# Five projections of a second layer as block products, and what then stands beside its banded attention

## The reference

```
h    = rmsnorm(x, norm1_g);  proj = h @ w_in
qa, ka, va, qm, km, vm, om, gm, mg = split(proj)     # 512,128,128, 512,512,512,512, 16, 2048
ya   = windowed_gqa(rmsnorm(qa)*gain/8, rmsnorm(ka)*gain, va, bias, sink)   # 8 heads of 64, 2 kv heads,
                                                     # 128 queries against the blocks before, at, after
qm,km = silu(conv5(concat(qm, km)) + b)              # 5 taps along the tokens, one channel at a time
ym   = rmsnorm(mlstm_fwd(qm,km,vm,gm) + mlstm_bwd(...)) * sigmoid(om)
g    = sigmoid(mg + merge_b)
x    = x + (g[:1024]*(ya @ w_branch_attn) + g[1024:]*(ym @ w_branch_mlstm)) @ w_out
x    = x + moe(rmsnorm(x))                           # 32 experts, two a token
```

## Time and profile before

| | |
|---|---|
| median of three runs | 1687.57 us |
| the profiled execution | 1688.09 us |
| its span, first to last instruction | 1686.3 us |
| mean granted TensorE clock | 0.993 |
| PE busy | 1630.7 us (97%) |
| DVE busy | 737.4 us (44%) |
| ACT, POOL busy | 387.8 (23%), 192.5 us (11%) |
| chain that ended last | PE 87%, DMA 8%, DVE 2% |

### The profile page before, as it was taken

One profiled execution on the slowest core, in us unless ns is written; L12 is line 12 of the kernel. 1 busy time (PEld: TensorE's weight loads), 2 busy tenths in 40 slices (PEclk: granted clock), 3 DMA queues, 4 the chain that ended last, 5 costly groups with the idle time before them and its releaser, 6 DMA issues.

```text
span 1686.3 us, 18096 instructions
## 1 busy us (share of the span) xinstructions
PE 1630.7 (97%) x7006; PEld 947.7 (56%) x7006; DVE 737.4 (44%) x1526; ACT 387.8 (23%) x823; POOL 192.5 (11%) x206
## 2 busy tenths in 40 slices
PE   7999999999999999999999999999999999997986
PEld 4444454578888888875444678744633333333332
DVE  3387786455454535451677256325521121121211
ACT  4443663510000000022365224100511111111110
POOL 1000000000000000010000424115022222221221
PEclk9999999999999999999999999999999999999999
DMA  5531114030222222223111111636899999999996
GB/s 189 125 75 50 51 51 140 11 113 0 100 78 72 100 100 75 106 66 117 50 50 50 51 50 51 206 97 234 352 394 417 416 418 417 424 413 417 422 416 235
DMA packets 75138, 303.63 MB, mean 180 GB/s; under 512 B 13037, under 2 KB 14194, under 8 KB 62124
## 3 DMA queue, kind: packets, MB, share of 16 engines
q1 hardware_dynamic: 64432, 287.40, 43.3%
q0 software_dynamic: 9872, 12.91, 3.7%
q10 hardware_dynamic: 748, 2.15, 0.3%
HBM read 306.99 MB, written 15.73 MB: 191 GB/s over the span
## 4 chain that ended last, share of the span: by engine, by line
PE 87%; DMA 8%; DVE 2%; SPq 2%; issue 1%; ACT 0%; POOL 0%; POOLq 0%; DVEq 0%; ACTq 0%
PE ps L1216 11%; PE ps L1260 11%; PE ps L1665 11%; PE ps L1084 9%; PE ps L1357 7%; PE ps L1504 6%; PE ps L1682 5%; DMA W<-in_w_expert_up 5%; PE ps L1120 3%; PE ps L1080 3%; PE ps L1543 3%; PE ps L1569 3%; DMA W<-in_w_expert_down 2%; PE ps L1368 2%; PE ps L1139 1%; SPq L766 1%
## 5 line engine op out<-in xcount | busy, mean ns | idle before, releaser
L3017 DVE SCALAR_TENSOR_TENSOR smb<-smb,ptb,ps 64x512 f32<-64x512 f32 x34 | 38.2, 1124 | 273.9 <-ACT smb L2139 273.9
L1084 PE MATMUL ps<-W 128*128 128x512 f32 (+1 forms) x336 | 149.3, 596 | 1.9 <-DMA W<-in_w_in 1.9
L1665 PE MATMUL ps<-W,cmask 128*64 128x512 f32 x480 | 132.5, 609 | 4.6 <-DMA W<-in_w_expert_up 3.9
L1665 PE MATMUL ps<-W,gb 128*64 128x512 f32 x480 | 129.5, 599 | 2.8 <-DMA W<-in_w_expert_up 2.7
L1357 PE MATMUL ps<-W 128*128 128x512 f32 x272 | 122.3, 599 | 1.9 <-DVE yT L2657 1.9
L1216 PE MATMUL ps<-yT,W 128*128 128x256 f32 x512 | 113.0, 379 | 0.0
L1682 PE MATMUL ps<-W,ptb 128*64 128x512 f32 x464 | 106.0, 598 | 4.2 <-DVE ptb L3023 3.3
L1260 PE MATMUL ps<-W,mix 128*128 128x256 f32 x496 | 108.5, 379 | 0.0
L1216 PEld LDWEIGHTS ps<-yT,W 128*128 128x128 f32 x512 | 97.3, 190 | 13.2
L1084 PEld LDWEIGHTS ps<-W 128*128 128x128 f32 (+1 forms) x336 | 61.2, 188 | 75.3 <-issue 72.9
L1260 PEld LDWEIGHTS ps<-W,mix 128*128 128x128 f32 x496 | 94.3, 190 | 12.8
(11 more groups left out here) (479 smaller groups left out, 2433.4 us busy)
## 6 DMA issues: line engine op xcount, KB each, us to landing
W<-in_w_expert_up SPq DMA_DIRECT2D x25, 2048.0 KB, 34.8
W<-in_w_expert_down SPq DMA_DIRECT2D x24, 2048.0 KB, 33.4
W<-in_w_expert_gate SPq DMA_DIRECT2D x22, 2048.0 KB, 32.0
W<-in_w_in SPq DMA_DIRECT2D x16, 2048.0 KB, 7.7
W<-in_w_up SPq DMA_DIRECT2D x8, 2048.0 KB, 8.3
W<-in_w_down SPq DMA_DIRECT2D x8, 2048.0 KB, 7.7
W<-in_w_out SPq DMA_DIRECT2D x4, 2048.0 KB, 7.8
W<-in_w_expert_gate SPq DMA_DIRECT2D x8, 1024.0 KB, 21.8
```

Of the source, the lines that this page charges most:

```text
L1084: ins = pe.matmul(ps[0:n, bank, :], wv[:, k, j * P:j * P + n], hT[:, k, :], start=(k == 0), stop=(k == KT - 1))
L1665: ins = pe.matmul(ps[64 * part:64 * part + 64, 2, :], xsT[s][:, k, :], w[part][:, k, :], start=(k == 0), stop=(k == KT - 1))
```

## The change

Nine projections (QM, KM, QA, VM, OM, and the four merge ones) now share one list of 63 block products, numbered `n`, and the names begin with `side_`: `side_product`, `side_keep`, `side_post`, `side_w_sums` and `side_h_sum` do what those with `gate_` did. `G2` keeps only `va2` (2) and `knorm`. Products 0 to 24 (QM, KM, QA, and four products of VM) come before the attention, `N_AHEAD = 25`; the other ten (VM's last three and OM) stand beside its steps; 35 to 62 are the merge ones, where they were. The convolutions and the gate scans now stand on DVE among the posts of products 4 to 18, and the first tap of each convolution is on ACT (`tap`), a copy with a scale. The roots of the query norms are taken of 16 columns a pair of chunks: `pair_sums` sums the squares to one column a head and tile of tokens, `pair_std` and `pair_recip` work on them, and `spread_roots` spreads the reciprocals over the partitions. The keys keep the old way. The `hT` sums now live in `x`, so `x` is stored to HBM after the norm and loaded again after the last product. Two small loads at the start of the kernel move under another semaphore.

```diff
+        side_h = [parts(x[:, n, :]) for n in range(4)]
+        early_w = [parts(flat(ptb[:, :, :])), parts(flat(yT[:, 6:8, :]))]
+        gate_w = [[parts(flat(smb[:, 2 * n:2 * n + 2, :])) for n in range(2)] + [parts(flat(yT[:, 4:6, :]))],
...
+        side_tmp = 3 * [[mix[:, 0, 512:1024], mix[:, 1, 512:1024], mix[:, 2, 512:1024], mix[:, 0, 0:512]]]
+        side_tmp += 2 * [[stage[:, 1, 0:512], stage[:, 1, 512:1024], stage[:, 0, 0:512], stage[:, 0, 512:1024]]]
+        side_tmp += 2 * [[yT[:, 0, :], yT[:, 1, :], yT[:, 2, :], R[:, 15376:15888]]]
+        side_tmp += 2 * [[R[:, 8208 + 512 * n:8720 + 512 * n] for n in range(4)]]
+        side_out = [convin[:, 0:4, 2:514], convin[:, 4:8, 2:514], qT, None, sigT] + [gate_view(c) for c in range(4)]
...
-                   ((VM, 512), (KVA2, 256), (QA2, 512), (QM, 512), (KM, 512), (OM, 512))]
+                   ((KVA2, 256), (QM, 512), (KM, 512), (QA2, 512), (VM, 512), (OM, 512))]
...
-        G2 = [("vm", b, i) for i in range(NT)]
-        C_GATES = b + 1
-        G2 += [("knorm", b + 1, 0), ("va2", b + 1, 0), ("va2", b + 1, 1)]
-        G2 += [("qnorm", b + 2, c) for c in range(4)]
-        BESIDE = len(G2)
-        G2 += [("conv", b + 3, c) for c in range(4)] + [("conv", b + 4, c) for c in range(4)]
-        G2 += [("om", b + 5, c) for c in range(4)]
+        C_GATES = b
...
+        N_AHEAD = 25
+
         def beside(a):
-            n, steps = 2 * (len(G2) - BESIDE), len(PAIRS) + 3
-            return [(BESIDE + q // 2, q % 2) for q in range(n * a // steps, n * (a + 1) // steps)]
-
-        def whole(a):
-            return [n for n, part in beside(a) if part == 1]
...
+        def side_bank(n):
+            if n < N_AHEAD:
+                return 4 + n % 4
+            return 4 + n % 2 if n < 35 else 5 if n < 49 else 4 + (n - 49) % 4
+
+        X_KEPT = [48 if i == 1 else 32 for i in range(NT)]
+        CONV_AFTER = {4: 0, 6: 1, 8: 2, 10: 3, 12: 4, 14: 5, 16: 6, 18: 7}
...
+                    sp.wait_ge(turn_src, 4 * NORM[T_N1] + NT)
+                    for i in range(NT):
+                        sp.dma_start(x_dram[i * P:(i + 1) * P, :], x[:, i, :]).then_inc(x_load[i], 16)
...
+                    sp.wait_ge(side_read, 63)
+                    for i in range(NT):
+                        sp.wait_ge(x_load[i], X_KEPT[i])
+                        sp.dma_start(x[:, i, :], x_dram[i * P:(i + 1) * P, :]).then_inc(x_load[i], 16)
...
+            def side_w_sums(c, part):
+                wv = ring_view(C_SIDE + c, KT, 512)
                 a11, a12, a21, a22 = (wv[:, 4 * k:4 * k + 4, 256 * n:256 * n + 256] for n in range(2) for k in range(2))
-                s1_, s2_, s4_ = gate_w[c // 3]
-                pool.wait_ge(ring_load[(C_MERGE + c) % 2], 16 * ((C_MERGE + c) // 2 + 1))
-                if c in (1, 2):
-                    pool.wait_ge(gate_prod, 7 * c - 1)
-                pool.tensor_tensor(s1_, a21, a22, ALU.add).then_inc(w_sums, 1)
-                pool.wait_ge(w_sums, 64 + 4 * c + 1)
-                pool.tensor_tensor(s2_, s1_, a11, ALU.subtract).then_inc(w_sums, 1)
-                pool.wait_ge(w_sums, 64 + 4 * c + 2)
-                pool.tensor_tensor(s4_, a12, s2_, ALU.subtract).then_inc(w_sums, 1)
-                pool.wait_ge(gate_prod, 7 * c + 3)
-                pool.tensor_tensor(s1_, a11, a21, ALU.subtract).then_inc(w_sums, 1)
-                pool.wait_ge(w_sums, 64 + 4 * c + 4)
+                s1_, s2_, s4_ = early_w + [a12] if early_sums(c) else gate_w[(c - 5) // 3]
+                if part == 0:
...
+            pool.wait_ge(turn_evac, turned_by(T_N1, NT - 1))
+            side_h_sum(0, b12, b11)
+            side_h_sum(1, b22, side_h[0])
+            side_w_sums(0, 1)
+            side_h_sum(2, b22, b12)
+            side_w_sums(0, 2)
+            side_h_sum(3, side_h[1], b21)
+            for c in range(1, 5):
+                for part in range(3):
+                    side_w_sums(c, part)
...
+            def pair_sums(pair, bank):
+                pe.wait_ge(sq_done, 2 * pair + 3)
+                group(bank, hstd_done, pair + 2)
+                for q in range(2):
+                    for i in range(NT):
+                        ins = pe.matmul(ps[:, bank, 8 * q + 2 * i:8 * q + 2 * i + 2],
+                                        squares[:, q, i * P:(i + 1) * P], ones[:, 0:P:64],
+                                        start=True, stop=True)
+                ins.then_inc(ssb_done, 1)
+
+            def spread_roots(pair, banks):
+                pe.wait_ge(pair_roots, pair + 1)
+                for q, bank in enumerate(banks):
+                    group(bank, qkn_done, 2 * pair + q + 2)
+                    for i in range(NT):
+                        for h in range(2):
+                            at = 16 * pair + 8 * q + 2 * i + h
+                            ins = pe.matmul(ps[64 * h:64 * h + 64, bank, i * P:(i + 1) * P],
+                                            hrs[:, at:at + 1].broadcast_to([P, 64]), ident[:, :], start=True, stop=True)
+                    ins.then_inc(roots_spread, 1)
+
+            pe.wait_ge(turn_evac, turned_by(T_N1, 1))
+            side_product(0)
+            side_product(1)
+            turn(T_N1, [2])
+            dense(0)
+            turn(T_N1, [3])
+            pe.wait_ge(turn_evac, turned_by(T_N1, NT - 1))
+            dense(1)
+            dense(2)
+            side_product(2)
+            norm_sums(1)
+            for n in range(3, 7):
+                side_product(n)
+            gate_rows_out()
+            for n in range(7, 14):
+                side_product(n)
+            gate_columns()
+            for n in range(14, 23):
+                side_product(n)
+            pair_sums(0, 2)
+            side_product(23)
+            spread_roots(0, (0, 1))
+            side_product(24)
...
-                norm_sums()
...
+                    for n in beside(a):
+                        side_product(n)
+                    if a == 0:
+                        pair_sums(1, 7)
+                    if a == 1:
+                        spread_roots(1, (6, 7))
...
+            def tap(c):
+                act.wait_ge(side_read, 7 * (c // 4) + SIDE_READ["P4" if c % 4 > 1 else "P3"])
+                act.activation(qkT[:, c, :], convin[:, c, 0:512], ACT.Copy, scale=convw[:, c, 0:1]).then_inc(first_tap, 1)
...
+            def pair_std(pair, bank):
+                act.wait_ge(ssb_done, pair + 2)
+                act.activation(hstd[:, 16 * pair:16 * pair + 16], ps[:, bank, 0:16], ACT.Sqrt,
+                               bias=epsc[:, 0:1], scale=1.0 / HD).then_inc(hstd_done, 1)
...
+            def pair_recip(pair):
+                dve.wait_ge(hstd_done, pair + 2)
+                dve.reciprocal(hrs[:, 16 * pair:16 * pair + 16], hstd[:, 16 * pair:16 * pair + 16]).then_inc(pair_roots, 1)
+
+            def query_norm(c, bank):
+                dve.wait_ge(roots_spread, c + 1)
+                dve.scalar_tensor_tensor(out=qT[:, c, :], in0=qT[:, c, :], scalar=gqk[:, 0:1], in1=ps[:, bank, :],
+                                         op0=ALU.mult, op1=ALU.mult).then_inc(qkn_done, 1)
...
+            side_post(1)
+            dense(0)
+            dense(1)
+            side_post(3)
+            key_norm()
+            for n in range(4, 20):
+                side_post(n)
+                if n in CONV_AFTER:
+                    conv(CONV_AFTER[n])
+                if n == 6:
+                    gate_scans()
+                if n == 13:
+                    gate_cols()
+            side_post(20)
+            pair_recip(0)
+            side_post(22)
+            query_norm(0, 0)
+            query_norm(1, 1)
+            side_post(24)
```

More of the change, by code:

```diff
@@ L49 @@
 NBLK = -(-SEQ // BLK)
-N_SMALL = 15
+N_SMALL = 17
 MAXJOBS = 2 * SEQ // BLK
@@ L546, in build @@
             chunk_done[C_WO + half] = (y_done, 7 + half)
-            for br_ in range(2):
-                chunk_done[C_MERGE + 2 * half + br_] = (gate_prod, 7 * (2 * half + br_ + 1))
             chunk_done[C_MERGE + 4 + half] = (y_done, 8 + 4 * (half + 1))
+        for c in range(9):
+            chunk_done[C_SIDE + c] = (side_prod, 7 * (c + 1))
         PRODUCTS = ("P1", "P2", "P5", "P6", "P3", "P7", "P4")
@@ L1460, in window_pairs @@
                         scores(a)
-                    for n, part in beside(a):
-                        dense(n, (part,))
+                    for n in beside(a):
[4 more added lines that the diff above has]
+                        spread_roots(1, (6, 7))
             window_pairs()
@@ L2001, in window_pairs @@
                         exps(a)
-                    for n in whole(a):
-                        dense(n)
+                    for n in beside(a):
+                        side_keep(n)
+                    if a == 0:
+                        pair_std(1, 7)
             window_pairs()
@@ L2676, in _, with conv @@
-            for n in range(BESIDE):
-                dense(n)
+            def conv(at):
```

(29 more changed lines are left out.)

520 lines of the change are left out of this document (235 added, 285 removed).

## The result

The changed kernel took 1702.45 us (median of four, 1697.62 to 1708.2) against 1686.93 of the kernel before (1685.78 to 1687.7): a ratio of 1.0094 [1.006, 1.0128], with the 95% interval in brackets. It is slower by 15.5 us, where I forecast 1684.7 and a range of 1677.5 to 1692. The profiled execution took 1708.2 us, span 1706.4, so it is the slowest of the four and its parts sum to some 6 us more than the median's.

What follows compares the result with a forecast made beforehand. TensorE was taken as the bound in the changed stretches: 11.9 us less work, minus 3.3, 1.5 and 12.4 of waits, with 8 or so of old waits gone, left a 2.9 us gain, 1684.7 us, range 1677.5 to 1692.

Steps and rivals of the forecast that it cites:

- TensorE's own work: Five projections as block products save 16.4 us, query norms cost 4.5 more: 11.9 us less; first stretch 109.8 us.
- Wait 1, the turn: First stretch, around the second `va2`: TensorE waits for the last norm and VectorE's copies, 3.3 us.
- Wait 2, the bank: First stretch: product 12 waits for its bank if GpSimd sums hold up VectorE's taps; 1.5 us taken, 3.1 laid out.
- B: Rival: GpSimd hold-ups in full, 3.1 us at the bank and 7.1 in the attention; 1687.9 us, no change; chance 0.20.
- The hold-ups in the attention: Four GpSimd sums may hold up VectorE's scalings in the attention: between 0 and 9.4 us, 3.0 taken.
- The start and lead terms: Attention: 10.2 us from its start through first step work, and 4.5 us where TensorE's products or values come late.
- the steps of 3.2 to 3.7: Attention: VectorE and ACT's loop sets steps 2 to 14, five at 3.23 and eight at 3.70, 45.8 us.
- the 12.4 at the end: End of the attention: last scaling 3.2, transposes 0.4, then product, values, product 8.8; 12.4 us.
- The branch weights: Reloading `x` ahead of their second half adds 5.4 us at 388 GB/s: 0.3 late at most, 0 taken.
- Experts move as a block: Last stretch: loads are issued when TensorE reaches given points, so an earlier start is passed on one to one.
- C: Rival: the attention's bare steps are longer, 0.5 us in each of 14, 7 us; 1691.7 us, slower; chance 0.20.
- A: Rival: cover holds, neither taps nor scalings held up and half the lead term gone; 1678.0 us; chance 0.20.

Runs made afterwards that it cites:

- experiment 11: The changed kernel with the first five projections' GpSimd sums in four pieces and `x` reloaded behind the branch weights, 25 products ahead: 1686.98 us, 0.9996.
- experiment 9: The changed kernel with seven matmuls whose result nobody reads put ahead of product 12, where TensorE waited: 1700.29 us, one run.
- before: The kernel without the change, which the changed kernel is compared with: 1686.93 us.
- experiment 10: The changed kernel with only the gate scans one projection later, behind the post of product 13 in place of 6: 1701.03 us, 1.0075.
- after: The changed kernel itself, with no further edits: 1702.45 us, 1.0094 against the kernel without the change.
- experiment 6: The kernel without the change, given four more GpSimd sums of 128 x 1024 beside its attention, their result not read: 1690.75 us, 1.0015.
- experiment 1: The changed kernel with the GpSimd sums of the first five projections and `hT` made over 8 of 256 columns, the rest left out: 1686.59 us, 1.0001.
- experiment 7: The changed kernel with early GpSimd sums over 8 of 256 columns and `x` reloaded behind the branch weights, 25 products ahead: 1681.9 us, 0.9966.
- experiment 2: The changed kernel with the reload of `x` moved behind the branch weights on SP's queue: 1697.74 us, 1.0065.
- experiment 8: The changed kernel with 22 products ahead, early sums in four pieces, `x` reloaded last and gate scans one projection later: 1684.32 us, 0.9978.
- experiment 4: The changed kernel with 22 products ahead of the attention in place of 25: 1689.61 us, 1.0015.
- experiment 5: The changed kernel with 22 products ahead, early GpSimd sums in four pieces and `x` reloaded behind the branch weights: 1681.44 us, 0.9962.
- experiment 3: The changed kernel with each weight sum of the first five projections made as four GpSimd instructions of a quarter: 1690.89 us, 1.0019.

## Why the prediction was wrong

**TensorE's own work: right.** A product takes 3.45 us, 110.4 us are busy in the first stretch at full clock (experiment 11; I had 109.8), and the pairs of norms take 1.68 and 1.90 for 2.0 and 1.96.

**Wait 1, the turn: right in sum, otherwise divided.** TensorE waits 1.4 us ahead of product 0, which I didn't have, then 0.3 for the last norm (1.65 in my working) and 1.3 ahead of the second `va2` (1.6): 3.0 for 3.3. Because product 0 began late, less was left to wait for the norm, whose last operation took 2.70 and ended at 758.05 as I had it. The clock stays at 1.00 behind these three.

**Wait 2, the bank: laid out right, taken wrong.** I had laid out 3.1 us for held-up taps and took 1.5, "half way between free and this". It was 2.95. The taps L2704 took up to 2.83 us (median 0.752) and the first scan 2.65. Half way between two mechanisms is a number that neither gives. The rule that I had cited from the Trainium skill, SBUF — State Buffer, section Who interferes with whom, gave 3.1, and these rows now show it for the taps as well. What the same section of the Trainium skill has of operations with one SBUF input (`tensor_scalar` can take the shared pair in some modes) fits the scalings of 4.77 us. One such row stood in the earlier trace rows already: the norm's operation there is of this kind (`TENSOR_SCALAR`) and took 2.70 us beside GpSimd's memset, where the same one took 0.75 for other tiles.

**The step that failed: what a wait costs.** In every term I counted a wait as its own length. No term had the clock. It is 0.50, 0.51, 0.83 and 0.73 in the windows at the four places that the change made TensorE wait longest. Behind product 12's wait it cost 3.3 us (10.16 for 6.90), of which experiment 9 gave back 2.5 net by filling the rest. In the attention, scores took 1.5 us more (2.37 for 0.92), two products 2.35 and 1.9 more (5.8 and 5.33 for 3.45), and behind the branch wait eight calls of the branches took 5.28 for 3.60. That is 10.7 us of the 23.0 by which the profiled execution missed the forecast. Waits longer than mine are some 9.5 (1.5 at the bank, 3.5 for the scalings, 4.6 for the branch weights), and 3.0 stand at the router, of which more below. The earlier trace rows show a clock of 1.00 in the two stretches that are changed, and I took it from there. But the trace of before has the price a little later, in the mLSTM, and I did not look for it (PE's timeline, then the window behind the wait):

```profile
987.05 3.49 PE L1416 MATMUL ps<-W 128*128 128x129 f32 x20 [2.75 <-DVE mix L2745]
990.33 4.30 PE L1504 MATMUL ps<-W 128*128 128x256 f32 x16
```
```profile
987.00:992.00 5.00, 4.95 (x25) 4.69 (x26) 0.50 (x1) 0.00 (x0) 0.00 (x0) 0.66 0.88 335
```

The same 20 and 16 matmuls take 2.40 and 3.62 elsewhere in that stage, so 2.75 us of rest cost 1.8 more. From this one row each of my waits near 3 us would have been priced at 1.65 times its length, and B, which was laid out, as well above no change. It would still have been a rough price: 1.5 us followed the rest of 3.9 in experiment 10 (a product of 5.12 for 3.62), 3.3 the one of 2.95 in after, and the rest of 1.95 shown under experiment 6 cost nothing in before. My "TensorE never rests" had passed over that one. The Trainium skill, TensorE: Matmul & The Clock Gate, section HAM oscillation — how this bites in real kernels, says that a kernel which rests again and again between groups of matmuls pays for the return to full clock each time; experiment 9 agrees for a single rest, with 1.00 for 0.50. I had not weighed it.

**The hold-ups in the attention: mis-sized.** I took 3.0 us, with B's 7.1 as its bound. By the table the attention was 9.0 above my schedule, clock included, so 12.0 stand in place of the 3.0; TensorE's waits for scalings (6.5) and the clock behind them (5.75) make 12.2. I had called the sums' place random ("begin anywhere"). But a sum is released by a product: the one at 879.84 starts 0.2 us after a product of TensorE ends, and the scaling of the bare step starts 0.1 after that. I read this as a place that the code's order sets; no run moved the sums alone.

**With the holds short, the schedule holds.** Experiment 11 leaves the order of the work and shortens only holds and the reload: its attention begins at 858.9 and ends at 940.0, where I had 859.3 and 939.5. The start and lead terms, the steps of 3.2 to 3.7, and the 12.4 at the end need no change in sum. I read this as support for the layout, not as proof of each term. My 80.2 held 3.0 of hold-ups, and experiment 1, with almost none, took 79.6 where 77.2 are left: so 2.4 us are in no term of mine.

**The branch weights: wrong.** I took 5.4 us for 2 MB at 388 GB/s and so 0.3 late at most. The landing grew by 8.9 us (23.0 for 14.1) and the issue came 0.5 later after the branches' start; less 5.1 of slack that is 4.3, and 4.6 was measured. The 388 GB/s were of the expert stage, where the stream is steady. Here the DMA engines were full between 1110 and 1120 us (shares of 1.02 and 1.07) and moved 220 and 190 GB/s. Why the rate was so low was not tried. Experiment 7 shows the cost, 4.7 us.

**Experts move as a block: right within what can be told.** From the output projection on, the profiled executions took 548.9 us before and 553.0 after, and 548.0 to 554.6 in the experiments. A part of this spread is the clock again. Behind the router TensorE rests 1.61 us in every kernel, and then 16 matmuls (L1734 in after) take 3.65 us in before and in experiments 2, 6, 7 and 8, 5.06 to 5.35 in 1, 4, 5 and 11, and 6.54 to 6.64 in after, 3, 9 and 10. The first group needs 548.0 to 548.9 us for the whole stretch, experiment 7 excepted (551.3), the other two 550.1 to 554.6. None of the edits touches this place, so what follows a rest differs from one execution to the next, by up to 3 us here.

**The rivals.** B named the mechanism, with the bank's 3.1 exact; its 1687.9 was 14.5 too low because it too left out the clock and the branch weights. C, slower by a longer loop of bare steps, is at most the 2.4 us named above: experiment 11 has these steps and ends 0.5 late. A (1678.0) had no holds at all and half the lead term; with the holds shortened, experiment 11 took 1686.98. The 16 us that go with the sums' length are divided between waiting and clock above by the rows of one execution; experiment 9 tests this at one of the four places only, in one run, 2.95 of waiting to 2.5 net of clock.

## What to carry to other kernels

Where TensorE rests between bursts, count the rest as itself and add what a lower clock behind it may cost (nothing to 3.3 us for rests of 1.3 to 4.6 us here), and first of all ask whether something useful can be moved into it. Moving products or posts ahead of a latency-bound stage takes its cover away; before doing so, look which long operations of a helper engine are released by exactly the work that remains in it, and cut them into pieces. Here the same rewriting was worth -6.2 us or +15.5 us by three small choices: how much stands beside the attention, how long one GpSimd sum is, and what is ahead of the branch weights on the queue.

## What the runs showed of the hardware

- A rest of 2.95 us on TensorE was followed by a granted clock of 0.50 over the next 4 us; one filled with matmuls was not (1.00).
- The same rest has no fixed price: behind 1.61 us of it at the router the same 16 matmuls took 3.65, 5.1 to 5.4 or 6.5 to 6.6 us in different executions.
- The clock was also 0.66 behind 6 us of small matmuls with no wait over 0.2 us (experiment 5).
- VectorE operations that read only SBUF were held up by a GpSimd sum whatever their size: 128 x 2 elements took 2.31 us beside it in experiment 6 (0.16 alone), the scan 2.65, a tap 2.83, two scalings 4.77. Two copies out of PSUM (L2715), the second of them beside a sum, took 1.27 us, as they do alone.
- The hold lasts for the length of one GpSimd instruction: with sums of a quarter the taps' longest was 1.32 us and their median 1.10 (experiment 5), against 2.83 and 0.752 in after. More taps are touched, each by less, and TensorE's waits shrink.
